# Adding the down sums in halves of 64 rows, each behind its own TensorE event

## The reference, cut to what matters

```python
h2 = rms_norm(x, ln2_g[l])
x = x + jnp.square(jax.nn.relu(h2 @ w_up[l])) @ w_down[l]
```

## Time and profile before

| | us |
|---|---|
| median of three runs | 654.97 |
| the three runs | 662.98, 654.57, 654.97 |
| the profiled execution | 654.6 |
| its span in the trace | 652.8 |
| PE busy | 638.7 |
| DVE, ACT, POOL busy | 496.7, 393.2, 137.4 |

### The profile page before, as it was taken

How to read it: one execution, slowest core, us unless ns; L and a number is a source line. 1 busy time by engine, 2 the same in 40 slices (tenths; PEclk the granted TensorE clock), 3 DMA queues, 4 the chain that set the end, 5 groups by cost and what they waited for, 6 DMA issues and landing times.

```text
span 652.8 us, 11733 instructions
## 1 busy us (share of the span) xinstructions
PE 638.7 (98%) x4189; PEld 565.9 (87%) x4189; DVE 496.7 (76%) x915; ACT 393.2 (60%) x784; POOL 137.4 (21%) x197
## 2 busy tenths in 40 slices
PE   8999999999999999998999999999999999999998
PEld 5999888888789888887999999999998778888886
DVE  5656756589887878897885677677668989999773
ACT  6554665467897647656446656756556654656750
POOL 1526755434321202112111011110111101100000
PEclk9999999999999999999999999999999999999999
DMA  7383538998989955994373897878978597866762
GB/s 282 127 325 110 204 119 323 300 284 212 270 231 286 348 174 178 279 282 102 65 194 104 212 262 212 222 227 222 269 195 209 163 225 219 214 212 223 228 194 97
DMA packets 33420, 140.40 MB, mean 215 GB/s; under 512 B 4584, under 2 KB 4968, under 8 KB 32402
## 3 DMA queue, kind: packets, MB, share of 16 engines
q1 hardware_dynamic: 22114, 81.63, 35.9%
q0 software_dynamic: 9696, 34.88, 27.7%
q10 hardware_dynamic: 1552, 23.14, 9.4%
HBM read 137.48 MB, written 65.06 MB: 310 GB/s over the span
## 4 chain that ended last, share of the span: by engine, by line
PE 78%; DVE 8%; DMA 5%; ACT 5%; issue 3%; ACTq 0%; DVEq 0%
PE bank L2043 13%; PE bank L2045 13%; PE bank L2044 13%; PE bank L2063 7%; PE bank L2460 5%; PE bank L2462 5%; PE bank L2461 5%; PE bank L2295 3%; DMA raw<-w_pairs 2%; PE bank L2238 2%; PE bank L2277 2%; PE bank L2390 2%; PE bank L2391 2%; PE bank L2392 2%; DMA raw<-down_sums 1%
## 5 line engine op out<-in xcount | busy, mean ns | idle before, releaser
L1337 DVE TENSOR_TENSOR w_lo<-raw,w_hi 128x1024 fp32r<-128x1024 f32 (+3 forms) x70 | 79.8, 1160 | 32.4 <-ACT w_hi L929 32.4
L929 ACT ACTIVATE w_hi<-raw 128x1024 fp32r<-128x1024 f32 (+3 forms) x70 | 67.5, 991 | 41.7 <-DMA raw<-w_pairs 34.1
L2043 PE MATMUL bank<-w_hi,act_hi 128*128 128x512 f32 (+3 forms) x224 | 89.4, 399 | 2.1 <-DVE act_lo L1351 0.9
L2045 PE MATMUL bank<-w_hi,act_lo 128*128 128x512 f32 (+3 forms) x224 | 79.8, 356 | 0.0
L2044 PE MATMUL bank<-w_lo,act_hi 128*128 128x512 f32 (+3 forms) x224 | 79.7, 356 | 0.0
L1065 ACT ACTIVATE p_buf<-s_buf,stats 128x128 f32<-128x128 f32 (+3 forms) x96 | 53.8, 561 | 32.5 <-PE bank L2063 18.1
L840 POOL DMA_DIRECT2D down_sums<-w_down x32 | 26.3, 912 | 210.6 <-PE bank L2462 143.3
L2043 PE MATMUL bank<-w_hi,s_all 128*128 128x512 f32 x140 | 54.7, 390 | 0.0
L2044 PE MATMUL bank<-w_lo,s_all 128*128 128x512 f32 x140 | 54.5, 389 | 0.0
L2045 PE MATMUL bank<-w_hi,s_all 128*128 128x512 f32 x140 | 54.5, 389 | 0.0
L2043 PEld LDWEIGHTS bank<-w_hi,act_hi 128*128 128x128 f32 x224 | 42.2, 188 | 10.2 <-issue 2.6
(11 more groups left out here) (313 smaller groups left out, 1830.8 us busy)
## 6 DMA issues: line engine op xcount, KB each, us to landing
down_sums<-w_down ACTq DMA_DIRECT2D x32, 512.0 KB, 6.0
down_sums<-w_down POOLq DMA_DIRECT2D x32, 512.0 KB, 7.7
raw<-down_sums SPq DMA_DIRECT2D x32, 512.0 KB, 4.4
up_sums<-w_pairs POOLq DMA_DIRECT2D x28, 512.0 KB, 9.6
raw<-up_sums SPq DMA_DIRECT2D x28, 512.0 KB, 5.0
raw<-weights SPq DMA_DIRECT2D x26, 512.0 KB, 6.1
up_sums<-w_pairs SPq DMA_DIRECT2D x16, 512.0 KB, 6.7
raw<-w_down SPq DMA_DIRECT2D x16, 512.0 KB, 4.5
```

Of the source, the lines that this page charges most:

```text
L929: ins = act.activation(hi[:, 0:width], raw[:, n % RAW, 0:width], ACT.Copy)
L1337: ins = dve.tensor_tensor(lo[:, 0:width], raw[:, n % RAW, 0:width], hi[:, 0:width].bitcast(F32), ALU.subtract)
L2043: pe.matmul(dst, a_h, w_h, start=start, stop=False, skip_group_check=onto)
L2045: return pe.matmul(dst, a_l, w_h, start=False, stop=stop, skip_group_check=onto)
```

## The change

Each add becomes two DMAs of 64 rows (256 KB). Both count on the same semaphore, and whoever waits for sum k waits for both. In the pairs, half 0 of sum p waits for event A of pair p and half 1 for event B: one sum a pair, 14 in all. The other 18 sums are 36 halves, and half h waits for the end of job 1 + (h - 28) * 5 // 4, which gives jobs 1, 2, 3, 4, 6, 7, 8, 9, 11 and so on up to 43 and 44. The loads, the copies and all work of PE, ACT and DVE stand as before, in the same order.

```diff
-            def add_down(k):
+            def add_down(k, half):
 
                 m, step = SUM_JOBS[k]
                 pool.wait_ge(*sum_copied[k // 8].at(8 * (k // 8) + 7))
                 if k >= 4:
                     pool.wait_ge(*sum_added[k % 4].at(k - 4))
-                pool.dma_start(sums_dram[k], a["w_down"][SUMS[m][1], step], accum_op=ALU.add,
-                               max_dma_last_dim=4096).then_inc(*sum_added[k % 4].mark(k))
+                rows_ = slice(64 * half, 64 * half + 64)
+                pool.dma_start(sums_dram[k, rows_], a["w_down"][SUMS[m][1], step, rows_], accum_op=ALU.add,
+                               max_dma_last_dim=4096).then_inc(*sum_added[k % 4].mark(k if half else (k, 0)))
...
-            for k in range(len(SUM_JOBS)):
-                p, i = 2 * k // 3, (k - 3 * PAIRS // 2) * 2 // 3
-                pool.wait_ge(*(dense_done.at(("A", p)) if p < PAIRS else job_used.at(JOB_AT["m2", i])))
-                add_down(k)
+            def add_half(h):
+
+                add_down(h // 2, h % 2)
+
+            for p in range(PAIRS):
+                pool.wait_ge(*dense_done.at(("A", p)))
+                add_half(2 * p)
+                pool.wait_ge(*dense_done.at(("B", p)))
+                add_half(2 * p + 1)
+            for h in range(2 * PAIRS, 2 * len(SUM_JOBS)):
+                pool.wait_ge(*job_free(1 + (h - 2 * PAIRS) * 5 // 4))
+                add_half(h)
```

## The result

| | before | changed |
|---|---|---|
| median of 11 runs, us | 655.23 (654.35 to 662.98) | 650.16 (649.4 to 652.01) |
| profiled execution, us | 654.6 | 649.47 |
| its span, us | 652.8 | 647.2 |

The ratio of the changed kernel to the one before is 0.9924, with a 95% interval of 0.9902 to 0.9947: it is 5.1 us faster. The ratios are taken over undisturbed executions, so they need not equal the quotient of the medians. Against the bound of 2% this is no measurable change, as forecast, but the interval is narrow enough to tell it from nothing.

What follows compares the result with a forecast made beforehand. TensorE was taken as the bound, busy 638.7 of 652.8 us, so only its idle gaps could return: -1.75 - 0.65 - 0.62 + 0.5 = -2.5 us, giving 652.5 us; range 651.1 to 656.8.

Steps and rivals of the forecast that it cites:

- The pairs, -1.75 us: Pair stage: ScalarE's P wait falls to near 2.3 us, so gaps of 0.56, 0.52 and 0.67 us go; bound 0.
- The passage, -0.65 us: From pairs to jobs: half of the 1.31 us in gaps of 0.93 and 0.38 us comes back; bounds 0 and -1.31.
- The first group of jobs, -0.62 us: Jobs to about 584 us: without bursts of adds the gap of 0.62 us vanishes; bounds 0 and -0.62.
- The second group, +0.5 us: Jobs from 584 to 650 us: 13 halves now run beside sum loads, a small toll; bounds 0 and +13.6.
- The starving rival: Second group of jobs: halves push load landing above 5.5 us and PE starves; 657.8 us, far end 668.6; chance 0.18.
- The issue, 64 for 32: GpSimd: 32 more DMA instructions cost 26 us of its time, but it sat idle, so this costs nothing.
- No gain: Rival, in the pairs: P meets part of a half every time, ScalarE waits some 3.3 us; 655.0 us; chance 0.22.

Runs made afterwards that it cites:

- pairs_only2: Against the changed kernel: pairs kept, the other 18 sums added whole, two at a time behind jobs 1, 6, 11 to 41; 655.71 us, ratio 1.0007.
- jobs_only2: Against the kernel before: pairs kept with 21 whole adds, the last 11 sums in halves over jobs 1 to 25; 654.36 us, ratio 0.9986.
- double_late2: Against the changed kernel: one more 64-row add into already read sums beside each half behind jobs 29 to 44; 658.68 us, ratio 1.0054.
- tiny_adds: Against the changed kernel: each half adds one row instead of 64, at the same events, sums left unfinished; 649.36 us, ratio 0.9913.
- whole_pairs: Against the changed kernel: one whole add behind event A of each pair, jobs still in halves; 650.04 us, ratio 0.9932.
- halves_bunched: Against the kernel before: each add split into two 64-row halves, issued back to back behind the old event; 653.57 us, ratio 0.9983.
- whole_paced: Against the kernel before: whole adds, one behind A of each pair and 18 behind jobs 1, 3, 6 to 43; 651.75 us, ratio 0.9951.

## Why the prediction was right in its mechanism and wrong in its size

The profiled executions differ by 654.6 - 649.47 = 5.1 us, and by 5.6 in span; the forecast was 2.5. Three steps of the sum failed: a gap was priced at its bracket alone, the passage was given back only by half, and the second group was charged a toll that it did not take. Point by point:

- **The pairs, -1.75 us: right, mis-sized.** The P waits fell to 1.8 to 2.9 us and the three gaps went. From the first to the last A event (356.81 to 490.57 before, 356.64 to 487.68 after) PE gained 2.72 us. The step that failed was reading the price of a gap off its brackets: the pairs with the three gaps lost 0.81, 0.78 and 0.92 us, 0.25 each beside the bracket, and a fourth pair lost 0.22 that shows in no bracket. One premise was wrong and did no harm: that the A half is gone when the P load goes out. With P in time that load goes out earlier too, not 5.7 us after A but 3.7 (timeline of SP; the A event is at 417.12), while the A half landed 5.1 us after its issue. The two overlap for some 1.4 us, and ACT's wait was 2.69 us all the same.

```profile
420.84 0.33 SPq L715 DMA_DIRECT2D raw<-w_pairs  x1
```

- **The passage, -0.65 us: wrong.** I took half of 1.31 because the chain was engine work without slack. All of it went; that chain starts with a late P load, and with the load in time it starts earlier and is done. pairs_only2 has the changed pairs and no gap at the passage, jobs_only2 the pairs of before and both gaps, the one of 0.38 without the load of 8.19 us to which I had also traced it. A chain of busy engines behind one late transfer isn't a bound of its own. With 0.25 for each of the two gaps this term is -1.8.
- **The first group of jobs, -0.62 us: right**, but for the 0.24 us more.
- **The second group, +0.5 us: wrong, the toll is nothing.** The demand of 2.78 us a job against 2.72 was mis-sized. The queues from 590 to 620 us (packets, MB, share) give 1.37 us for each of 11.0 loads, where I had 1.66, and 1.51 for each of 9.2 halves, where I had 1.4:

```profile
q1 hardware_dynamic: 1581, 5.76, 50.3%
q0 software_dynamic: 744, 2.40, 46.2%
```

  That is 1.37 + 0.8 x 1.51 = 2.6 us a job, just below PE's pace, and the lead stayed at 2.5 us. The landing of 5.3 us was just below the 5.5 at which it would have shrunk. The starving rival (657.8 us) named the right place: double_late2 with 658.7 is that rival, brought about with 13 more halves, and pairs_only2 shows it with the same bytes in bursts. That the two times are so near is luck, since the rival had reckoned with single halves.
- **The sum.** 3.68 of gaps and 1.73 beside them are 5.41 us, measured from the first A event to the last matmul; the remaining 0.17 of the 5.58 lies before the first add and is nothing of the change. From the forecast of 2.52 to 5.41 it is 1.73 for the price of the gaps, 0.66 for the other half of the passage and 0.5 for the toll.
- **The range** ended at 651.1 for the same reason: "655.0 - 3.68, all six gaps gone" was taken for a floor. The floor was 655.2 - 5.6, 649.6, and tiny_adds measured 649.4.
- **The issue, 64 for 32: right.** 0.78 us each, and POOL waited before each of them.
- **No gain** (0.22) was wrong: the B half did not delay P, and whole_pairs shows that it isn't needed either.

What is not settled is how late P lands with the same adds. What a late split costs is known to 0.02 us (above, at halves_bunched), but the kernel before and jobs_only2 lost 2.72 and 3.23 us in the same pairs, in one profiled execution each; so it stays open whether four halves in place of two whole adds let P in sooner.

## What to carry to other kernels

When an engine is busy 98% of the span, list its gaps one by one, follow each to a transfer, and price it from the distances of the starts and not from the brackets, which leave out what the pipeline loses in stopping and starting and show nothing of short stalls. Background transfers should be given out at the pace of the work, one piece per event, and not in bursts: what decides is how many of them are in flight when the urgent load goes out, and how much lead the consumer has there. Before moving background work to a stretch that had none, work out the demand per step against its pace; at 98% it may still be free, but 2.5 us of lead is then all the margin.

## What the runs showed of the hardware that I had not expected

A long gap lowers PE's clock. After the gap of 3.33 us in pairs_only2, the granted clock fell from 1.00 to 0.50, the level of 1.2 GHz, within a microsecond after PE had started again, and stayed there for about three (windows; the clock is the third number from the end):

```profile
608.00:609.00 1.00, 0.61 (x2) 0.52 (x3) 1.00 (x3) 1.00 (x2) 0.00 (x0) 0.90 0.05 20
609.00:610.00 1.00, 1.00 (x4) 0.80 (x3) 1.00 (x2) 1.00 (x2) 0.00 (x0) 0.50 0.85 242
612.00:613.00 1.00, 1.00 (x5) 0.86 (x4) 0.84 (x2) 1.00 (x2) 0.00 (x0) 0.90 0.82 307
```

Matmuls of 512 columns started 0.43 us apart there and 0.23 at the higher level, and seven such intervals, 1.4 us more than at full clock, are the greater part of the 2.50 us beside the gaps of that kernel. The gap of 1.94 us in double_late2 did the same (0.50 from 620 to 621 us); gaps of up to 1.2 us after 340 us did not. In whole_paced the clock also stood at 0.83 from 300 to 310 us, ahead of the adds, in a stretch where PE idled for 0.94 us; the kernel before idled as long there at 1.00, and no row shows what set the two apart. The Trainium skill (TensorE: Matmul & The Clock Gate, Part 1) has a monitor set the clock by how busy PE has lately been; the rows after the two long gaps agree.

Half the bytes is not half the latency, nor less latency at all. From 350 to 480 us a half landed in 5.2 us at the median in the changed kernel, and a whole add, alone behind its A event in whole_pairs, in 5.3 (in this order):

```profile
DMA to landing us min/median/max: 4.4/5.2/7.2
...
DMA to landing us min/median/max: 5.1/5.3/6.6
```

The whole adds of the kernel before, two thirds of them in twos, took 7.4 us in that stretch: company, and not size, made them slow.
